# A two-layer hybrid decoder step: weights and token tiles of the next phase made in the one before, and a regrouped sample part

## What is computed

```python
mod = silu(c) @ w_ada[l] + b_ada[l]; shift, scale, gate = split(mod, 3)
h = rms_norm(x, g_pre[l]) * (1 + scale) + shift
# layer 0
gq, gk, gv, gz, glr, rq, rk, rv, rz = split(h @ w_in)
o, s = chunked_gated_linear_attn(q, k, v, lg, s0)        # chunks of 64
y = (concat(rms_norm(o_g), group_norm(o_r)) * silu(z)) @ w_out
# layer 1
qkv, z, b_raw, a_raw = split(h @ w_in)                   # 3072, 1024, 8, 8
buf = concat([s_conv, qkv]); conv = sum(buf[:, i:i + T] * conv_w[i] for i in range(4))
new_conv = buf[:, -3:]; q, k, v = split(silu(conv))
beta = sigmoid(b_raw); log_g = -exp(a_log) * softplus(a_raw + dt_bias)
o, s = chunked_gated_delta(l2norm(q), l2norm(k), v, beta, log_g, s0)
y = (rms_norm(o) * silu(z)) @ w_out
# both
x = x + gate * rms_norm(y, g_post[l])
```

## Time and profile before

| | us |
|---|---|
| median of the runs | 2886.0 |
| the profiled execution | 2881.07 |
| its span, first to last instruction | 2879.3 |
| first DMA issue of the first mixing phase | 713.27 |
| of the second projection | 1136.97 |
| of the second mixing phase | 1975.79 |
| TensorE busy, all of the span | 2598.7 |
| a `w_out_ab` piece: high half on ScalarE, low half on POOL | 1.06, 2.12 |
| a piece of the second projection's weights: issue to landing, high half, low half on POOL | 4.6, 1.04, 2.56 |

### The profile page before, as it was taken

One profiled execution on the slowest core, in us unless ns is written; L12 is line 12 of the kernel. 1 busy time (PEld: TensorE's weight loads), 2 busy tenths in 40 slices (PEclk: granted clock), 3 DMA queues, 4 the chain that ended last, 5 costly groups with the idle time before them and its releaser, 6 DMA issues. The chain is left out here.

```text
span 2879.3 us, 55037 instructions
## 1 busy us (share of the span) xinstructions
PE 2598.7 (90%) x21400; PEld 1536.3 (53%) x21400; DVE 1361.7 (47%) x3074; ACT 930.4 (32%) x2709; POOL 768.7 (27%) x845
## 2 busy tenths in 40 slices
PE   7989999997599997698999999984899999999997
PEld 2334444444356542343444444453778787878783
DVE  3220313110377853694462635543566666666635
ACT  2532323222111110443231222214545454545431
POOL 1330101000311110354010000002664646565531
PEclk9899999999699997799999999996999999999977
DMA  7341212011664442454111111116322222222212
GB/s 265 114 141 43 88 37 77 30 66 59 180 223 156 147 135 88 111 157 125 52 60 55 62 63 45 56 36 175 98 83 76 83 75 83 77 80 87 56 38 73
DMA packets 264269, 270.37 MB, mean 94 GB/s; under 512 B 32126, under 2 KB 199438, under 8 KB 264015
## 3 DMA queue, kind: packets, MB, share of 16 engines
q1 hardware_dynamic: 185948, 219.50, 23.6%
q10 hardware_dynamic: 78112, 47.87, 6.1%
HBM read 179.96 MB, written 87.36 MB: 93 GB/s over the span
## 5 line engine op out<-in xcount | busy, mean ns | idle before, releaser
L518 PE MATMUL inc_b<-inc_h,inc_w_hi 128*128 128x512 bf16 (+3 forms) x1920 | 484.1, 347 | 26.2 <-DVE inc_h L462 15.6
L518 PE MATMUL inab_b<-inab_wt,inab_h 128*128 128x512 f16 (+1 forms) x1632 | 361.2, 384 | 13.0 <-POOL inab_wt L498 13.0
L518 PE MATMUL inc_b<-inc_h,inc_w_lo 128*128 128x512 bf16 (+1 forms) x960 | 314.5, 346 | 0.0
L518 PEld LDWEIGHTS inc_b<-inc_h,inc_w_hi 128*128 128x128 f16 x1920 | 169.8, 99 | 211.3 <-DVE inc_h L462 16.3
L518 PEld LDWEIGHTS inab_b<-inab_wt,inab_h 128*128 128x128 bf16 (+3 forms) x1632 | 162.2, 100 | 210.1 <-issue 25.4
L518 PE MATMUL inc_b<-inc_w_hi,inc_h 128*128 128x512 f16 (+3 forms) x816 | 176.2, 313 | 15.0 <-POOL inc_w_lo L498 14.3
L518 PE MATMUL inab_b<-inab_h,inab_wc_hi 128*128 128x512 bf16 (+3 forms) x720 | 181.0, 346 | 8.9 <-DVE inab_h L462 8.0
L1770 DVE SCALAR_TENSOR_TENSOR inc_acc<-inc_ub,inc_taps,inc_acc 128x512 f32<-128x512 f32 (+1 forms) x240 | 167.5, 698 | 8.6
L1685 ACT ACTIVATE inc_ub<-inc_b 128x512 f32<-128x512 f32 x96 | 57.3, 597 | 312.7 <-PE inc_b L518 312.7
L518 PEld LDWEIGHTS inc_b<-inc_h,inc_w_lo 128*128 128x128 f16 x960 | 93.7, 99 | 92.8 <-issue 3.8
L768 ACT ACTIVATE inab_vz<-inab_b 128x512 f32<-128x512 f32 (+1 forms) x68 | 40.6, 597 | 288.2 <-PE inab_b L518 284.5
(11 more groups left out here) (403 smaller groups left out, 5428.2 us busy)
## 6 DMA issues: line engine op xcount, KB each, us to landing
tmp_qkv<-inc_so SPq DMA_DIRECT2D x96, 256.0 KB, 2.0
mixc_qkv<-tmp_qkv SPq DMA_DIRECT2D x15, 1536.0 KB, 7.7
inc_stage<-in_w_in_c ACTq DMA_DIRECT2D x32, 512.0 KB, 4.6
inab_wt<-in_w_ada SPq DMA_DIRECT2D x6, 2048.0 KB, 10.7
inab_stage<-in_w_in_ab ACTq DMA_DIRECT2D x24, 512.0 KB, 4.3
mixab_cw<-in_w_ada ACTq DMA_DIRECT2D x6, 2048.0 KB, 8.7
inab_x<-in_x_prompt SPq DMA_DIRECT2D x16, 512.0 KB, 5.0
tmp_v<-inab_vz SPq DMA_DIRECT2D x32, 256.0 KB, 3.6
```

Source lines behind the costliest of these rows:

```text
L518: last = nc.tensor.matmul(dst, lhs(a, k), rhs(b, k), start=(k == 0 and i == 0), stop=(k == KT - 1 and i == len(PASSES) - 1))
```

## The change

1. **Output weights of the first mixing phase.** A class `RowWeights` loads and splits `w_out_ab` in the last block (units 0 to 3, after groups 16, 19, 22, 25) and the sample part (units 4 to 7) of the first projection: load and high half on ScalarE, low half on POOL. They lie in `keep32`, a room of 8 x 1024 float32 columns that outlives the phases and is otherwise `Prep`'s `x`, `xn`, `hf` and `h_next`. `Finish` takes them from there. The state loads move behind the tile loop, and the ring of `w_ada` buffers in the mixing phase has two places instead of three.
2. **First four token tiles of the second projection.** A class `Early` loads, squares, norms (ScalarE now) and transposes them in the sample part of the first mixing phase, keeps them raw in `raw_next`, and scales and splits them once layer 1's scales are there. The second projection starts with `raw_next` as its `h`; its first four turns of `Prep` are gone, POOL makes the first four low halves of weights. The two halves of `h` now alternate in runs of 512 (`halves`).
3. **Sample part of the second projection.** The 27 groups become one `ab` product, three products of 1024 channels and one of 1024 gate columns (`pair`): the 64 sample rows are the stationary operand, 64 columns wide, and two products of 512 columns go to PSUM rows 0 to 63 and 64 to 127. The results are copied, transposed back (`turned`), and convolved 8 channels at a time. The prompt's last convolution rows are transposed in the last block (`tail`), the sample's are stored by 18 DMAs straight from the copied products.

```diff
+class RowWeights:
+    def __init__(self, ph, src, keep, stage, free):
+        self.src, self.stage, self.free = src, stage, free
+        room = keep[:].bitcast(F16).rearrange("p (u e n) -> p u e n", u=KT, e=2)
+        self.w = [room[:, :, e, :] for e in range(2)]
+        self.stage_in = [ph.sem(f"row_in{i}") for i in range(2)]
+        self.hi_done, self.lo_done = ph.sem("row_hi"), ph.sem("row_lo")
+    def load(self, eng, u):
+        if u < KT:
+            wait(eng, self.lo_done, u - 1)
+            eng.dma_start(self.stage[u % 2], self.src[u * P:(u + 1) * P, :]).then_inc(self.stage_in[u % 2], 16)
+    def hi(self, act, u):
+        act.wait_ge(*self.free[u // 4])
+        self.load(act, u + 1)
+        act.wait_ge(self.stage_in[u % 2], 16 * (u // 2 + 1))
+        act.activation(self.w[0][:, u, :], self.stage[u % 2], ACT.Copy).then_inc(self.hi_done, 1)
+    def lo(self, pool, u):
+        pool.wait_ge(self.hi_done, u + 1)
+        pool.tensor_tensor(self.w[1][:, u, :], self.stage[u % 2], self.w[0][:, u, :], ALU.subtract).then_inc(self.lo_done, 1)
...
-    return [flat.bitcast(dt).rearrange("p (e k n) -> p e k n", e=2, k=k)[:, e] for e, dt in enumerate((BF16, F16))]
+    return [flat.bitcast(dt).rearrange("p (k e n) -> p k e n", e=2, k=k)[:, :, e] for e, dt in enumerate((BF16, F16))]
...
+        rows_out.load(act, 0)
+        groups(nb - 1, BLK, [(nt, NS)], rows_at={16: 0, 19: 1, 22: 2, 25: 3})
+        groups(nb, NS, [], rows_at={4: 4, 10: 5, 14: 6, 16: 7})
...
+    def turn(self, pe, t):
+        pe.wait_ge(self.xnd, t + 1)
+        wait(pe, self.done, t)
+        for k in range(KT):
+            last = self.nc.tensor.transpose(self.banks[k // 4][:, (k % 4) * P:(k % 4 + 1) * P], self.xn[:, k * P:(k + 1) * P], self.ident)
+        last.then_inc(self.tr, 1)
+    def take(self, act, t):
+        act.wait_ge(self.tr, t + 1)
+        for i in range(2):
+            last = act.activation(self.raw[:, 4 * i:4 * i + 4, t * P:(t + 1) * P], self.banks[i][:].rearrange("p (k n) -> p k n", n=P), ACT.Copy)
+        last.then_inc(self.done, 1)
+    def scale_low(self, act):
+        act.wait_ge(self.modT_ready, 1)
+        act.wait_ge(self.done, TPB)
+        def scaled(k):
+            wait(act, self.lo_p, k // 2 - 1)
+            act.activation(self.tmp[k % 4], self.raw[:, k, :], ACT.Identity, bias=self.m[:, k, 0:1], scale=self.m[:, 8 + k, 0:1]
+                           ).then_inc(self.m_a, 1)
+        scaled(0)
+        for k in range(KT):
+            if k % 2 == 0 and k + 2 < KT:
+                scaled(k + 2)
+            act.wait_ge(self.m_v if k % 2 else self.m_a, k // 2 + 1)
+            act.activation(self.h[0][:, k, :], self.tmp[k % 4], ACT.Copy).then_inc(self.hi, 1)
+    def scale_high(self, dve):
+        dve.wait_ge(self.modT_ready, 1)
+        dve.wait_ge(self.done, TPB)
+        def scaled(k):
+            wait(dve, self.lo_v, k // 2 - 1)
+            dve.tensor_scalar(self.tmp[k % 4], self.raw[:, k, :], self.m[:, 8 + k, 0:1], self.m[:, k, 0:1], ALU.mult, ALU.add
+                              ).then_inc(self.m_v, 1)
+        scaled(1)
+        for k in (1, 3, 5, 7):
+            if k + 2 < KT:
+                scaled(k + 2)
+            dve.wait_ge(self.hi, k + 1)
+            dve.tensor_tensor(self.h[1][:, k, :], self.tmp[k % 4], self.h[0][:, k, :], ALU.subtract).then_inc(self.lo_v, 1)
+    def scale_rest(self, pool):
+        for k in (0, 2, 4, 6):
...
-        sp.wait_ge(fin.weights.lo_done, D // P)
-        for p in range(PAIRS):
-            sp.dma_start(Ss[p][:], state_rows("state", p, True)).then_inc(sm_in, 16)
...
+        for p in range(PAIRS):
+            sp.dma_start(Ss[p][:], state_rows("state", p, True)).then_inc(sm_in, 16)
...
-            if early == 0:
-                for u in range(4):
-                    fin.weights.hi(act, u)
...
-        for n in range(Cond.RING):
+        for n in range(2):
...
-        cond.load(act, 3)
+        cond.load(act, 2)
         fin.square(act, nt - 1, P, 0)
         fin.square(act, nt - 1, P, 1)
         ktok_copy(nt, NS)
+        early.load(act, 0)
+        cond.load(act, 3)
         cond.load(act, 4)
+        early.square(act, 0)
+        oT_copy(nt, NS)
         cond.load(act, 5)
-        oT_copy(nt, NS)
+        def first_tile(t):
+            if t:
+                early.square(act, t)
+            early.norm(act, t)
+            if t + 1 < TPB:
+                early.load(act, t + 1)
+            early.take(act, t)
+        for t in range(TPB - 1):
+            first_tile(t)
+        early.square(act, TPB - 1)
+        early.norm(act, TPB - 1)
         cond.take(act)
         cond.gates(act)
+        early.take(act, TPB - 1)
+        early.scale_low(act)
         fin.square(act, nt, NS, 0)
         fin.square(act, nt, NS, 1)
@@ -1373,6 +1520,7 @@
             if p < 2:
                 by_sequence(p + 2)
                 cond.add(dve, 4 + p)
+        early.scale_high(dve)
         dve.wait_ge(gate_in, 32)
         fin.gated_add(dve, nt, 0, nt // 2, NS)
...
         pe.wait_ge(oT_ready, nt + 1)
         for p in range(PAIRS):
+            early.turn(pe, p)
             pe.wait_ge(vm_ready, p + 1)
...
-        for t in range(2):
-            prep.load(sp, t, t, P)
+        prep.first_tiles_done(sp)
         load_tables(sp, tab_in, tab, names, io["table"])
...
-        for t in range(TPB):
-            sp.wait_ge(prep.xnd, t + 1)
-            prep.load(sp, t + 2, t % 2, P)
+        for t in range(TPB, TPB + 2):
...
+        def tail(k):
+            pe.wait_ge(conv_done, 2 + NCH * nb)
+            wait(pe, tail_ready, 2 * k)
+            for c in range(8 * k, 8 * k + 8):
+                last = nc.tensor.transpose(ext[c // 4 % 2][0:CONV - 1, (c % 4) * P:(c % 4 + 1) * P], halo[:, c, :], ident)
+            last.then_inc(tail_turned, 1)
...
+        h_s = lambda e, k: prep.h[e][:, k, 0:NS]
+        product(nc, bank[0][0:NS, 0:16], h_s, lambda e, k: W[e][:, k, N_C - 16:N_C]).then_inc(s_ab, 1)
+        def pair(dst, c0):
+            for k in range(KT):
+                for i, (a, b) in enumerate(PASSES):
+                    for half in range(2):
+                        last = nc.tensor.matmul(dst[half * NS:(half + 1) * NS, :], h_s(a, k),
+                                                W[b][:, k, c0 + half * 512:c0 + (half + 1) * 512],
+                                                start=(k == 0 and i == 0), stop=(k == KT - 1 and i == len(PASSES) - 1))
+            return last
+        def turned(j):
+            pe.wait_ge(ut_ready, j + 1)
+            if j == 0:
+                pe.wait_ge(halo_ready, 1)
+            if j == 1:
+                pe.wait_ge(ab_ready, 1)
+            for i in range(4):
+                for half in range(2):
+                    rows = slice(half * NS, (half + 1) * NS)
+                    last = nc.tensor.transpose(turn_bank[j][half][:, i * NS:(i + 1) * NS], ut[j][rows, i * P:(i + 1) * P], ident[rows, rows])
+            last.then_inc(s_turned, 1)
+        pe.wait_ge(tail_ready, 6)
+        for j in range(2):
+            pair(pair_bank[j], j * 1024).then_inc(s_mm, 1)
+        turned(0)
+        pair(pair_bank[2], 2 * 1024).then_inc(s_mm, 1)
+        turned(1)
+        pair(bank[2], 3 * 1024).then_inc(s_z, 1)
+        turned(2)
+        pe.wait_ge(g_ready, 1)
+        pe.wait_ge(us_ready, 2)
+        nc.tensor.matmul(pst[0][:, 0:nt * H], tv["incl"], tmp[3][:, 0:nt, :], start=True, stop=True)
...
```

357 lines of the change are left out of this document (207 added, 150 removed).

## The result

| us | before | after |
|---|---|---|
| median of the runs beside each other | 2886.22 (2885.61 to 2886.76) | 2801.85 (2795.68 to 2804.41) |
| profiled execution, its span | 2881.07, 2879.3 | 2795.68, 2793.6 |
| first issue of the first mixing phase | 713.27 | 712.14 |
| of the second projection | 1136.97 | 1115.06 |
| of the second mixing phase | 1975.79 | 1887.56 |

The ratio is 0.9705, with a 95% interval from 0.9688 to 0.9721: 84.4 us faster by the medians, 85.7 by the spans. The forecast was 2794 in 2775 to 2820. A second session with the changed kernel gave 2807.99 against 2886.18, 78.2 less (ratio 0.9729 [0.9711, 0.9748]), so the gain is known to some 6 us. In what follows a place is told by its distance from its phase's first DMA issue, since the phases begin at other times in each execution.

What follows compares the result with a forecast made beforehand. TensorE was taken to set the time, idle or slow for 203 us in three phases divided by barriers. Edge gains of 28.6 + 35.1 + 28.0 = 91.7 us off the median 2886.0 gave 2794 us, range 2775 to 2820.

Steps and rivals of the forecast that it cites:

- Edge A, the norm: Start of the first mixing phase: VectorE's norm starts at 737.8 instead of 761.39, pieces made earlier; 23.6 us gained.
- Edge A, traffic: First mixing phase, tiles from 796.54: less w_ada and state traffic shortens early tiles, 6 us gained (0 to 7.2).
- Edge A, its price in the projection: End of the first projection: added pieces on ScalarE, POOL and the queues cost 1 us (0 to 4).
- Edge B, the first product: Start of second projection: first product 9.8 us after first issue, not 49.9, set by the taps; 40.1 us gained.
- Edge B, the sample part: End of the first mixing phase: making the four token tiles there costs 5 us in all (1 to 12).
- Copies: Copies of 128x4096 at block ends: new layout charged nothing; the rival case, chance 0.12: 7.8 not 2.35 us, +33.
- Edge C: End of second projection: sample pairs of 5.2 us, next phase at 1947.8 not 1975.8; 28.0 us gained (18 to 32).
- Weights in the first block: Second projection's first block: pieces every 4.1 us against 5.18 used; the rival, chance 0.02: weight feed bounds, 2898 us.

Runs made afterwards that it cites:

- part A undone: The changed kernel with the eight w_out_ab pieces loaded and split at the start of the first mixing phase again: 2824.54 us, ratio 0.9791.
- the run without it: The changed kernel with the first four token tiles made at the start of the second projection again, none in the mixing phase: 2835.52 us, ratio 0.9843.
- the edit of ScalarE's norm: The changed kernel with ScalarE's norm of the next phase's first tile, and its second load, ahead of the wait for the fifth w_ada load: 2798.68 us.
- the run with the halves in turn: The changed kernel with each sample pair's 24 products of one column half before the 24 of the other, not alternating: 2819.41 us, ratio 0.9772.

## Why the prediction was right, step by step

- **Edge A, the norm (23.6).** The gain is 22.4. That the norm, forecast for 737.8, is found at 737.82 is luck, since the phase began 1.1 us earlier in this execution and 10 later in another. The working held: the input time of VectorE plus the 2.4 us of a later tile. It left one thing out: the new code loads whole rows, and with part A undone the norm lies at 41.4, so about 16 of the 22.4 come from moving the pieces and 6.7, by the traces, from the shape of their loads.
- **Edge A, traffic (6).** From the norm to tile 6 the tiles gained 5.3, of which 4.3 in the steps from tile 3 to tile 5. Right in size, but by luck. The term named a third load of `w_ada` and the states. With part A undone and that traffic as light as now, 1.1 of the 5.3 is there. The states had landed before the small load was issued, and have no part in it. And 2.0 of the 7.2 us that the working counted as traffic were no wait but the same products at a granted clock of 0.89 instead of 1.00. The loads of `w_ada` do make the small load late: what is left (2.9) goes with one load more.
- **Edge A, its price in the projection (1).** None is seen: the phase ended 1.1 us earlier. But this is the phase that varies most: the changed kernel's second profile has it at 723.3 instead of 712.1, so a microsecond can't be read there.
- **Edge B, the first product (9.8 us; 40.1).** 10.5 and 39.4. The taps decide, as the working had it; their loads come at 7.8, and the transposes and one copy stand behind. What the working did not see is that this is mostly work.
- **Edge B, the sample part (5).** Mis-sized: 6.9, or 6.7 by the run without it. The late first norm was forecast as about 1 us and is 1.75 and then 0.74 more on the second tile (the edit of ScalarE's norm gives back 2.8). The transposes, forecast as 3.6 at full clock, took 4.9, because the fourth tile's run at about half the rate, in a stretch that was as slow before. The scaling and the squares, the places where I expected to pay most, cost nothing.
- **Copies.** 1.22 us for 4096 elements in either layout, nothing charged, nothing paid.
- **Edge C (28.0).** Pairs of 5.3 us, forecast 5.2. From the copy to the next phase 38.9 us, with 3.1 of transposes in front of the copy 42.0, which is the working's 42.0. By the rule of the Trainium skill ("TensorE: Matmul & The Clock Gate", Part 3, the mechanism) that a weight load overlaps running products only in another row group, the loads would have cost an estimated 19 us. The traces don't agree with it: neither the changed kernel nor the run with the halves in turn shows an exposed load. The same section also lets a load run ahead that goes to the background weight buffer, which the prediction did not weigh.
- **Weights in the first block.** The working had them come faster than they are used and named TensorE's waiting for them as a sign of being wrong. TensorE does wait, 16.9 us in two places, but 14.3 of that was there before. What the sum lacked is the 2.6.
- **What no term had.** From the first product to the last copy 4.2 us more: some 3.1 are the transposes that I had counted in C, waits for weights are 2.6 longer, and about 1.5 went the other way. The second mixing phase, 2.5 more, was not in the sum at all, and nearly all of it can be spread.

The differences from the working, in the marks: edge A with the first projection + 0.2 (27.7 + 1.1 against 28.6), the first product - 0.7, the sample part - 1.9, edge C 0, the stretch up to the last copy - 1.1 beyond its transposes, the second mixing phase - 2.5. That makes - 6.0, and 91.7 - 6.0 = 85.7 is the difference of the spans. By these two executions the gain was 7% smaller than forecast, and more than half of what it lacks lies in places that no term named. By the medians it was 8% smaller, in the second session 15%, so the single microseconds of this list hold for this pair of profiles.

## What to carry to other kernels

At a barrier, read what each engine waits for in the first tile, and ask which of it (weights, first inputs) could be made in the previous phase where an engine is idle and the queues are quiet; the gain is the whole of the edge, and such gains add (here 87.4 us by the parts, 87.1 by the two phases). Before calling a gap a wait, take out the engine's own work in it: moving 1.9 us of transposes gains nothing. Put an instruction that others wait for ahead of any issue that has to wait for a buffer on the same queue. And when a moved load is written anew, look whether its shape changed with it: part of the gain may be that.

## What the runs showed of the hardware that I had not expected

- Two products with 64 stationary columns, on the two column halves, run at nearly twice the rate if issued alternately: 5.3 against 9.65 us for the same 48, with the weight loads hidden in both.
- The granted clock falls with TensorE fully busy: 0.58 in 1087 to 1100, behind a row of f32 products with 9 columns of weights, and 0.75 in the first pairs of some executions and not of others. The executions of one kernel differ with it: the first mixing phase of the changed kernel began at 712.1 in one profile and at 723.3 in another, where the granted clock is 0.96 instead of 1.00 in 240 to 320, 360 to 400, 440 to 480 and 520 to 560.
- A small load takes 6.9 us from issue to landing with one load of 2 MB issued 6 us before it, 13.1 with two and 15.3 with three; TensorE then waits 0, 2.63 and 4.98 us for it. States of 2 MB that had landed 24 us before made no difference.
- Pieces of 512 KB in runs of 512 B and in whole rows of 4 KB, under the same other loads: the first landed 14.5 and 7.7 us after its issue.
